# Sums of squares and gate inputs as products with few weight columns and 256 moving tokens

## What is computed

```python
q = rms_norm(c_q, q_norm, 1e-6) @ w_uq          # latent of 384 columns
c_kv = rms_norm(c_kv, kv_norm, 1e-6)            # latent of 256 columns
...
xf * lax.rsqrt(jnp.mean(jnp.square(xf), -1, keepdims=True) + eps) * g
```

## Time and profile before

| | |
|---|---|
| median of 3 runs | 2110.95 us (2110.72 to 2112.76) |
| the profiled execution's own time | 2112.28 us |
| its span, first to last instruction | 2110.5 us |
| mean granted TensorE clock in it | 0.996 of full |
| busy: TensorE, VectorE, ScalarE | 2082.3, 1784.5, 1398.2 us |
| HBM traffic | 270 GB/s over the span |

### The profile page before, as it was taken

How to read it: one execution, slowest core, us unless ns; L and a number is a source line. 1 busy time by engine, 2 the same in 40 slices (tenths; PEclk the granted TensorE clock), 3 DMA queues, 4 the chain that set the end, 5 groups by cost and what they waited for, 6 DMA issues and landing times. The chain is left out here.

```text
span 2110.5 us, 28169 instructions
## 1 busy us (share of the span) xinstructions
PE 2082.3 (99%) x11028; PEld 1767.9 (84%) x11028; DVE 1784.5 (85%) x2350; ACT 1398.2 (66%) x1842; POOL 58.7 (3%) x56
## 2 busy tenths in 40 slices
PE   8999999999999999999999999999999999999999
PEld 7878888878888888888888888879988888888887
DVE  5776768789999999999999999988888878878887
ACT  5555546567888888888888888857654455465444
POOL 0011002001000000000000000000000000000000
PEclk9999999999999999999999999999999999999999
DMA  9447664559999999999999999944446555236552
GB/s 310 161 139 270 220 219 151 210 186 394 393 396 396 395 395 386 384 378 388 370 393 375 386 370 385 394 166 155 153 152 219 186 193 168 93 109 231 179 195 105
DMA packets 284668, 567.05 MB, mean 269 GB/s; under 512 B 9180, under 2 KB 113760, under 8 KB 284288
## 3 DMA queue, kind: packets, MB, share of 16 engines
q1 hardware_dynamic: 277936, 538.28, 70.7%
q0 software_dynamic: 5728, 23.73, 3.1%
q10 hardware_dynamic: 864, 3.15, 0.4%
HBM read 556.21 MB, written 12.59 MB: 270 GB/s over the span
## 5 line engine op out<-in xcount | busy, mean ns | idle before, releaser
L436 DVE TENSOR_TENSOR wl<-raw,wh 128x1024 fp32r<-128x1024 f32 (+1 forms) x632 | 763.7, 1243 | 106.3 <-ACT wh L428 100.3
L428 ACT ACTIVATE wh<-raw 128x1024 fp32r<-128x1024 f32 (+1 forms) x632 | 647.0, 1053 | 167.5 <-PE psum L473 60.5
L436 DVE TENSOR_TENSOR wl<-arena,wh 128x1024 fp32r<-128x1024 f32 x384 | 456.4, 1222 | 38.8 <-ACT wh L428 32.1
L428 ACT ACTIVATE wh<-arena 128x1024 fp32r<-128x1024 f32 x384 | 403.1, 1061 | 86.9 <-PE psum L473 81.5
L471 PE MATMUL psum<-wh,xhl 128*128 128x512 f32 (+1 forms) x1136 | 449.1, 395 | 2.0 <-DVE wl L436 0.8
L473 PE MATMUL psum<-wh,xhl 128*128 128x512 f32 (+1 forms) x1136 | 442.1, 389 | 0.0
L472 PE MATMUL psum<-wl,xhl 128*128 128x512 f32 (+1 forms) x1136 | 441.6, 389 | 0.0
L463 PE MATMUL psum<-xhl,wh 128*128 128x512 f32 x980 | 349.4, 396 | 0.0
L471 PE MATMUL psum<-wh,yh 128*128 128x512 f32 x752 | 295.3, 393 | 1.0 <-DVE yl L1572 1.0
L473 PE MATMUL psum<-wh,yl 128*128 128x512 f32 x752 | 292.9, 390 | 0.0
L472 PE MATMUL psum<-wl,yh 128*128 128x512 f32 x752 | 292.8, 389 | 0.0
(11 more groups left out here) (435 smaller groups left out, 2092.5 us busy)
## 6 DMA issues: line engine op xcount, KB each, us to landing
arena<-in_moe_g SPq DMA_DIRECT2D x72, 1024.0 KB, 9.3
arena<-in_moe_u SPq DMA_DIRECT2D x72, 1024.0 KB, 9.0
raw<-in_moe_d SPq DMA_DIRECT2D x64, 1024.0 KB, 9.4
arena<-in_moe_d SPq DMA_DIRECT2D x48, 1024.0 KB, 8.9
raw<-in_ff_up SPq DMA_DIRECT2D x48, 1024.0 KB, 5.2
raw<-in_moe_g SPq DMA_DIRECT2D x40, 1024.0 KB, 7.9
raw<-in_moe_u SPq DMA_DIRECT2D x40, 1024.0 KB, 9.5
raw<-in_ff_down SPq DMA_DIRECT2D x24, 1024.0 KB, 5.4
```

What stands on the lines that cost most here:

```text
L428: A.activation(unit(s, i)[0], raw_half(s, i), ACT.Copy).then_inc(*s.w_hi.tick(i))
L436: V.tensor_tensor(lo, raw_half(s, i), hi.bitcast(F), SUB).then_inc(*s.w_lo.tick(i))
```

## The change

The operands change sides. The weights are now constants with few columns (2 in the mixers, 8 in the window layer, 4 for the heads, the 8 gate columns themselves), each with ones in the column that its chunk adds to, and all 256 tokens of a chunk of squares (or of the input) move. The result has 2 to 8 partitions by 256 tokens. ScalarE copies it to a tile `COLS` in `SC` (one tile for all places), and two small products with a piece of the identity turn it to tokens on the partitions, into columns 256 and on of the same bank; for the gate inputs a further pair adds the bias. VectorE reads it there.

The products and the turns are two steps at different places of TensorE's order, with other work between, and the copy has its place in ScalarE's order. In each mixer the products stand one `dv` unit earlier; in the window layer the products of the keys stand one projection unit earlier, those of the first query heads ahead of `rope(0)` with the turns behind it, those of the others ahead of `weigh(0, 0)` with the turns behind. In the hybrid layer the head sums' products stand ahead of the last `oo` unit and the gate inputs' turns behind the first `q` unit; VectorE's second group of taps moves ahead of its read of the gate inputs. Three constants of 52 columns are added to the load of constants, which had 2883 columns.

```diff
@@ -24,7 +24,8 @@
 HEAD = [0, 2, 1, 3]
 GELU_C = math.sqrt(2.0 / math.pi)
 CONSTS = [("ident", 128), ("ones", 256), ("tri", 128), ("iota", 256), ("bd2", 2), ("rot", 128), ("anti", 128), ("fold", 128),
-          ("maskM", 256), ("maskW", 256), ("cos1", 256), ("oh", 384), ("sel4", 512), ("tri8", 64), ("invf", 1)]
+          ("maskM", 256), ("maskW", 256), ("cos1", 256), ("oh", 384), ("sel4", 512), ("tri8", 64), ("invf", 1),
+          ("colw", 32), ("colh", 16), ("colm", 4)]
 SMALLS = [("qn0", 3), ("qn1", 3), ("kvn0", 2), ("kvn1", 2), ("dn0", 1), ("dn1", 1),
           ("g10", 8), ("g11", 8), ("b10", 8), ("b11", 8), ("g20", 8), ("g21", 8), ("b20", 8), ("b21", 8),
           ("router", 64), ("nm0", 8), ("nm1", 8), ("nf0", 8), ("nf1", 8), ("np0", 8), ("np1", 8),
@@ -89,6 +90,13 @@
         s4[h, h] = 1
     put("sel4", s4.reshape(4, 512))
     put("tri8", np.tile((np.arange(8)[None, :] < np.arange(8)[:, None]).reshape(1, 64), (P, 1)))
+    pick = np.zeros((P, 4, 8))
+    for j in range(4):
+        pick[:64, j, 2 * j] = 1
+        pick[64:, j, 2 * j + 1] = 1
+    put("colw", pick.reshape(P, 32))
+    put("colh", np.tile(np.eye(4).reshape(1, 16), (P, 1)))
+    put("colm", np.tile(np.eye(2).reshape(1, 4), (P, 1)))
     half = np.float32(10000.0) ** (-np.arange(32, dtype=np.float32) * np.float32(2.0 / 64))
     put("invf", half.astype(np.float32)[d % 32][:, None])
     return c
@@ -598,7 +606,7 @@
         drained(i, (dve, name))
 
     def dve_scales(name, i, w, inv_n, eps, at=256):
-        ps = pair(i)
+        ps = pair(i)[:, 256:512]
         val, r, w1, w2 = (SC[:, o:o + 2 * w] for o in (at, at + 2 * w, at + 4 * w, at + 6 * w))
         V.wait_ge(*pe.of(name))
         if not isinstance(eps, (list, float)):
@@ -615,6 +623,30 @@
 
     def scales_at(w, at=256):
         return SC[:, at + 2 * w:at + 4 * w].rearrange("p (t n) -> p t n", t=2)
+
+    COLS = SC[0:8, 640:896]
+
+    def pe_cols(name, b, n, terms):
+        ps = take(b)
+        for i, (w, x) in enumerate(terms):
+            y = T.matmul(ps[0:n, 0:256], w, x, start=i == 0, stop=i == len(terms) - 1)
+        y.then_inc(*pe.tick(f"{name}.c"))
+
+    def act_cols(name, b, n):
+        A.wait_ge(*pe.of(f"{name}.c"))
+        A.activation(COLS[0:n, :], bk(b)[0:n, 0:256], ACT.Copy).then_inc(*act.tick(f"{name}.c"))
+
+    def pe_cols_turned(name, b, n, drain, plus=None):
+        T.wait_ge(*act.of(f"{name}.c"))
+        for t in range(2):
+            o, x = bk(b)[:, 256 + t * n:256 + (t + 1) * n], COLS[0:n, t * P:(t + 1) * P]
+            if plus is None:
+                y = T.transpose(o, x, ident[0:n, 0:n])
+            else:
+                T.matmul(o, x, ident[0:n, 0:n], start=True, stop=False)
+                y = T.matmul(o, plus[0], plus[1], start=False, stop=True)
+        y.then_inc(*pe.tick(name))
+        empties(b, (dve, drain))
 
     def spread(ps, r, n, hd):
         m = P // hd
@@ -1026,17 +1058,11 @@
                     for t in range(2):
                         x = step_b(pv[:, t * 512:(t + 1) * 512], at_t(XX, kk, t), tuple(q[:, k, :] for q in w), kk == 0, kk == 7)
                 x.then_inc(*pe.tick(("unit", u), f"{st}.dv"))
+                if (n, h) == (0, 1):
+                    T.wait_ge(*act.of(f"{st}.sq2"))
+                    pe_cols(f"{st}.ss", 1, 2, [(C("colm")[:, 2 * (c // 3):2 * (c // 3) + 2], SQC[:, c, :]) for c in range(5)])
                 if (n, h) == (1, 0):
-
-                    ps = take(1)
-                    T.wait_ge(*act.of(f"{st}.sq2"))
-                    for t in range(2):
-                        for i, chunks in enumerate(((0, 1, 2), (3, 4))):
-                            for c in chunks:
-                                x = T.matmul(ps[:, 2 * t + i:2 * t + i + 1], SQC[:, c, t * P:(t + 1) * P], ones[:, 0:1],
-                                             start=c == chunks[0], stop=c == chunks[-1])
-                    x.then_inc(*pe.tick(f"{st}.ss"))
-                    empties(1, (dve, f"{st}.ss"))
+                    pe_cols_turned(f"{st}.ss", 1, 2, f"{st}.ss")
                     T.wait_ge(*dve.of(f"{st}.E0"))
                     take(0)
                     turn_heads(DE[0][0], P, (0,), f"{st}.T0")
@@ -1226,6 +1252,7 @@
         hi_to(main, U + 19)
         latent(2, 6)
         hi_to(main, U + 21)
+        act_cols(f"{st}.ss", 1, 2)
         A.wait_ge(*pe.of(f"{st}.T0"))
         if l:
             A.wait_ge(*added_out.of("second"))
@@ -1375,7 +1402,7 @@
         V.wait_ge(*pe.of(f"{st}.ss"))
         val, r, w1, w2 = (SC[:, o:o + 4] for o in (256, 260, 264, 268))
         for n, (x, y) in enumerate(((192.0 / 384, 192e-6), (1.0 / 256, 1e-6))):
-            V.tensor_scalar(val.rearrange("p (t n) -> p t n", t=2)[:, :, n], bk(1)[:, 0:4].rearrange("p (t n) -> p t n", t=2)[:, :, n],
+            V.tensor_scalar(val.rearrange("p (t n) -> p t n", t=2)[:, :, n], bk(1)[:, 256:260].rearrange("p (t n) -> p t n", t=2)[:, :, n],
                             x, y, MUL, ADD).then_inc(*dve.tick(f"{st}.ss"))
         rsqrt(r, val, w1, w2)
         dve.name(f"{st}.ss.r")
@@ -2405,16 +2432,13 @@
 
         def gate_inputs():
 
-            ps, wif = claim(1), S("wif").rearrange("p (k n) -> p k n", k=8)
+            T.wait_ge(*act.of("nm0.k"))
+            wif = S("wif").rearrange("p (k n) -> p k n", k=8)
+            pe_cols("hy.if", 2, 8, [(wif[:, k, :], XT[:, k, :]) for k in range(8)])
+
+        def gate_inputs_turned():
             T.wait_ge(*dve.of("par"))
-            T.wait_ge(*act.of("nm0.k"))
-            for t in range(2):
-                o = ps[:, t * 8:(t + 1) * 8]
-                for k in range(8):
-                    T.matmul(o, XT[:, k, t * P:(t + 1) * P], wif[:, k, :], start=k == 0, stop=False)
-                x = T.matmul(o, ones[0:4, :], DIF, start=False, stop=True)
-            x.then_inc(*pe.tick("hy.if"))
-            drained(1, (dve, "hy.ifs"))
+            pe_cols_turned("hy.if", 2, 8, "hy.ifs", (ones[0:4, :], DIF))
 
         def gate_rows():
             ps = claim(1)
@@ -2486,7 +2510,7 @@
 
         def sums():
             T.wait_ge(*act.of("hy.sq"))
-            pe_sums("hy.ss", 2, [[AA[:, h, :]] for h in range(4)], False)
+            pe_cols("hy.ss", 4, 4, [(C("colh")[:, 4 * h:4 * h + 4], AA[:, h, :]) for h in range(4)])
 
         def norm():
             T.wait_ge(*dve.of("hy.ss.r"))
@@ -2498,7 +2522,7 @@
 
         proj(0, "xr", xw=by_blocks("nm0"))
         gate_inputs()
-        proj(2, "q")
+        proj(2, "q", (gate_inputs_turned,))
         gates()
         gate_rows()
         proj(2, "k", (None, None, rows_turned, spread_rows))
@@ -2518,8 +2542,8 @@
         drained(1, (dve, "hy.v"))
         turn(0, 3)
         turn(1, 2)
-        proj(0, "oo", (weigh,))
-        sums()
+        proj(0, "oo", (weigh, None, sums))
+        pe_cols_turned("hy.ss", 4, 4, "hy.ss")
         pe_project("hy", (1, 3), lambda kk: YY if kk < 4 else XX, halves("hyo"), {2: norm},
                    lambda t: pe_rows("nf0", ar(0, 2, 1024), NF, t, (lambda: pe_vector("nf1", 0)) if t else None), early=True)
         drained(1, (dve, "nf0.a01"))
@@ -2535,7 +2559,7 @@
                 A.activation(dst[:, c, :], pair(i)[:, c * 256:(c + 1) * 256], ACT.Identity, bias=bn[:, n0 + c:n0 + c + 1]
                              ).then_inc(*act.tick(f"hy.{name}"))
 
-        def conv(i, name, dst, src, n0, w, b, o):
+        def conv(i, name, dst, src, n0, w, b, o, beside=None):
 
             for p in range(2):
                 proj(i, name, src[:, o:o + 4, :], n0, (2 * p, 2 * p + 1))
@@ -2543,6 +2567,8 @@
                 for c in (o + 2 * p, o + 2 * p + 1):
                     A.activation(dst[:, c, :], src[:, c, :], ACT.Identity, scale=w[:, 3, c:c + 1], bias=b[:, c:c + 1]
                                  ).then_inc(*act.tick(f"hy.{name}t{p}"))
+                if p == 0 and beside is not None:
+                    beside()
 
         def conv_tanh(name, o, p):
             s = slice(o + 2 * p, o + 2 * p + 2)
@@ -2558,7 +2584,7 @@
 
         hi_to(main, u0 + 2)
         hi_to(main, u0 + 4)
-        conv(0, "xr", XC, XR, 0, rw, S("rcb"), 0)
+        conv(0, "xr", XC, XR, 0, rw, S("rcb"), 0, lambda: act_cols("hy.if", 2, 8))
         A.wait_ge(*dve.of("hy.ifa"))
         A.activation(IFE, IFW, ACT.Exp).then_inc(*act.tick("hy.ife"))
         hi_to(main, u0 + 6)
@@ -2613,6 +2639,7 @@
         A.wait_ge(*act.of("hy.mt1"))
         A.wait_ge(*dve.of("hy.aa"))
         A.activation(AA, MT[:, 4:8, :], ACT.Square).then_inc(*act.tick("hy.sq"))
+        act_cols("hy.ss", 4, 4)
         A.wait_ge(*pe.of("hy.oo"))
         for c in range(4):
             A.activation(OO[:, c, :], pair(0)[:, c * 256:(c + 1) * 256], ACT.Tanh, scale=0.5, bias=HBO[:, c:c + 1]
@@ -2687,12 +2714,12 @@
         lo_to(main, u0 + 4)
         V.wait_ge(*act.of("hy.xrt0"))
         taps(XC[:, 0, :], XR[:, 0, :], rw, 0, "hy.xc")
+        taps(XC[:, 1, :], XR[:, 1, :], rw, 1, "hy.xc")
         V.wait_ge(*pe.of("hy.if"))
```

(30 more changed lines are left out.)

## The result

| | before | after |
|---|---|---|
| median (6 runs each, side by side) | 2111.55 us (2109.26 to 2115.12) | 2117.99 us (2116.61 to 2120.07) |
| ratio, 95% interval | | 1.0029 (1.0019 to 1.0039) |
| profiled execution: own time, span | 2112.28, 2110.5 us | 2116.92, 2115.1 us |
| mean granted TensorE clock | 0.996 | 0.998 |

The account below looks back on a forecast made before the run. TensorE, busy 99% of the span, bounds the kernel; -1.3 - 3.2 + 0.2 + 0.15 + 3.1 + 0.1 = -0.95 us takes 2112.28 to 2111.3 us, likeliest 2112.3 with one fall in half the executions; range 2108.0 to 2115.5.

Parts of the forecast that it names:

- Prices: At each site of the new sums: a pair of turns with a pipe restart costs 0.2 us, bounded by 0.1 and 0.4.
- Falls of the clock in the mixers and gate inputs: First mixer's half-clock stretch goes, -1.7 us; gate inputs' goes too, within a change of -3.2 us there.
- rival D: Few weight columns hold the clock no better; falls stay in first mixer and gate inputs: 2114.7 to 2116.4 us, chance 0.08.
- somewhat under even odds: Chance given each of the window layer's two stalls of bringing 3.4 us at half clock, costing 1.7 us.
- the rule on short idles: Skill's rule that short idles between matmul groups swing the clock: both window stalls bring falls, 2114.7 us.
- rival C: Both window stalls bring falls, perhaps one more wait or fall later: 2114.7 or 2116.4 us, chance 0.17.
- First query heads: Window layer: TensorE stands 2.1 us for the key multiplication; mask 6.3 us after the sines, 2.3 us late.
- Second query heads: Window layer: TensorE stands 2.1 us for ScalarE's square; next head turn +3.55 us, whole window query part +3.1.
- Constants: 52 more columns in the early load of constants: +0.1 us.

Follow-up runs that it names:

- window_only: The kernel before with only the window layer's three sums changed (products, places, copies, turns): 2120.67 us, ratio 1.0036.
- bank1: The changed kernel with the first query heads' sums in bank 1 in place of bank 4: 2114.17 us, ratio 1.0006 to the kernel before.
- bank1_weigh: As bank1, with the second query heads' sums back behind the weighing and their turns behind the third head turn: 2114.13 us, ratio 1.0002 to the kernel before.
- rope_first: As bank1_weigh, with the rotations ahead of the first query heads' sums and the turns right behind those products: 2113.16 us, ratio 1.0005 to the kernel before.
- mixed: As rope_first, with the second query heads' sums made by the old products right behind the weighing: 2111.97 us, ratio 0.9996 to the kernel before.
- consts_only: The kernel before with only the 52 more constant columns, which nothing reads: executed once, time not read; its trace drifts by 0.47 us.
- gate_only: The kernel before with only the new gate inputs (eight products of 8 weight columns, copy, turns): 2111.04 us, ratio 0.9989.

## Why the prediction was wrong

The mechanism was right at most steps; several terms of the sum were too small, all on the same side. The step that failed most is the price of a site, 0.2 us, in which the second break was not counted. Beside it stand the reading of the window layer's second stall, a fall at a place that the sum did not have, and a drift that no term had.

- **Prices: wrong.** "With a restart of the pipe I take 0.2, bounded by 0.1 and 0.4" priced the turns and not the second break. At four of its seven sites (both mixers, gate inputs, head sums) the change breaks the stream of large products once more than before, and each such break costs 0.36 us beside the turns' 0.21. (The keys' products moved next to the rotations, so there the number of breaks is the same as before; why they cost +0.56 all the same stays open.) The second mixer measured +0.64 for a forecast of +0.2, the head sums +0.62 for 0.2, the keys +0.56 for 0.15; with the first mixer (+0.71) they missed by 1.8 us together, and one more break is half of the 0.7 us that the gate inputs gained less than forecast. Since the falls that went there were worth 3.4 us, the new form of the gate inputs costs about 0.9 us at full clock, an estimate from the ledger (3.4 less 2.54), for the forecast 0.2. Even my upper bound of 0.4 lay below the measured value.
- **Falls of the clock in the mixers and gate inputs: right at their places** (1.00 in both), and rival D is out. But the fall of the first mixer comes in three executions of five, so the change removes 1.0 us there on the mean, not 1.7, and pays 0.71 for it.
- **The fall at 1474 us: missed.** I gave the falls to the new stalls; both stalls of the changed kernel passed at full clock (its rows of eight records take 1.89 and 1.90 us). In all, one stall of the five of 1.7 to 2.5 us in the study's window layers was followed by a fall, and one of the thirteen at the bias table, where every wait of 2.8 to 3.4 us at 1409 us has one. So "somewhat under even odds" was too high for such a stall, and the rule on short idles, read so that each of the two brings a fall, is not borne out; rival C's mechanism was seen once, in `window_only`. The fall came at a place whose own code is unchanged and which has it in eight of twelve unsplit traces. The profile before was free of it; whether that was luck, or the new gate inputs ahead of it (seven of nine, for one of three) had a part, is open.
- **First query heads: right in kind.** Stall 2.47 us for 2.1, mask 6.25 us after the sines without idle for 6.3. The mask is 3.54 us late, of which 0.66 were there on entering the layer: 2.9 for the forecast 2.3. `bank1` takes the stall away and 2.5 us with it.
- **Second query heads: the stall right (1.71 for 2.1), its reading wrong.** I counted it as a cost. `bank1_weigh` took it away and gained 0.1 us; what costs is that the answer passes through ScalarE's queue (the copy at 1837.41 behind a drain) and two more places of TensorE's order, while VectorE is there for it at once (in `rope_first` it waits 1.08 us for the turns). `mixed` shows that the new form as a whole costs 1.2 us at this place; how much of it is ScalarE's part was not tried. The next head turn is 4.2 us late from entry for the forecast +3.55, the window part +3.97 for +3.1.
- **Constants: a term missing.** The columns cost 0.47 us on the way (`consts_only`), which the forecast did not have. The 0.27 us of the start can't be put down to them: `gate_only`, without these columns, has +0.37 there, and `bank1`, with them, -0.08.
- **The range: too narrow.** The terms missed by 0.9 (mixers), 0.7 (gates), 0.4, 0.4, 0.9 (window), 0.8 (constants, drift and the 0.14 ahead of the gates) and 1.5 (the fall), in sum 5.6 us, and none the other way. The measured median lies another 1.1 us above the profiled execution. I had widened the sum for the turns' bound and for falls, but not for a price missing at every site. Rival C had the right side for another reason.

## What to carry to other kernels

Count the places at which TensorE's stream changes between large and small products, not only the products: one more cost about 0.36 us here, so a small product divided into two steps must save more than that, and of the sites here only the gate inputs did, by the fall of the clock that went (there in three traces of three with the old form, in none of eleven with the new); at full clock they too cost more than before. Use the two-step form where its answer is not awaited; where another engine stands ready for it, the old products at one place were faster in the traces (`mixed`), even with a fall of the clock in the stretch. A stall of the bounding engine is a cost only if what it waits for is itself early enough afterwards: take it away in an experiment before counting it.

## What the runs showed of the hardware that I had not expected

- 52 constant columns that nothing reads made a kernel lose 0.47 us, evenly over some 900 us in which no instruction differs, in steps of about 0.015 us. What in the chip does it was not tried.
- Falls of the clock at a place come and go between executions and kernels with the same code there (three of five, five of eight, eight of twelve), away from the program's end always 3.4 us at 1.2 GHz or twice that. Two profiles can differ by luck as much as by the change, and the time has to be split into places before it is compared.
- Not only rows of products that move one to eight columns stand ahead of falls: 2.9 us of products with 4 rows were followed by one in eight traces of twelve, without a wait of TensorE.
- Waits of TensorE of 1.5 to 2.5 us were followed by a fall in 2 cases of 18, waits of 2.8 to 3.4 us at one place in 14 of 14.
